# Pooling stage: order of low parts, evictions and value tiles; end of the delta rule: places of the inverses, token halves of the first output tiles

## What is computed

```python
def rms_norm(x, g):
    xf = x.astype(jnp.float32)
    return xf * lax.rsqrt(jnp.mean(xf * xf, axis=-1, keepdims=True) + EPS) * g

def multiscale_pool(h, w_groups, scale):            # windows 2, 4, 8, 16, one for each 256 channels
    hf = h.reshape(B, L, POOL_GROUPS, POOL_G)
    ...                                             # d = mean over the last w tokens, less the token
    return jnp.einsum("blgc,gce->blge", d, w_groups).reshape(B, L, D) * scale

def gated_delta_rule(q, k, v, a, b, a_log, dt_bias):
    """S_t = a_t S_{t-1} (I - beta_t k_t k_t^T) + beta_t v_t k_t^T, o_t = S_t q_t (chunkwise form)."""
    ...
    sol = triangular_solve(lower + eye, rhs)        # rhs = [v * beta, k * beta * exp(G)], u, w = sol
    def step(state, xs):
        v_new = u_n - einsum("bhcd,bhde->bhce", w_n, state)
        o_n = einsum("bhcd,bhde->bhce", qg_n, state) + einsum("bhij,bhje->bhie", p_n, v_new)
        state = state * gl_n + einsum("bhcd,bhce->bhde", kg_n, v_new)
        return state, o_n

def second_block(x, mem, ...):
    mem_n = rms_norm(mem, mem_norm)
    u = rms_norm(h, norm_pre_mix)
    y_mix, q_mem = gdn_branch(u @ gdn_w_in, ...)    # delta rule, rms_norm of each head, times silu(z)
    mem_k, mem_v = jnp.split(mem_n @ w_mem_kv, 2, axis=-1)
    y_mem = memory_attention(q_mem, mem_k, mem_v)
    y = jnp.concatenate([y_mix, y_mem], axis=-1) @ w_out
    h = h + rms_norm(y, norm_post_mix)
    return h + rms_norm(swiglu(rms_norm(h, norm_pre_ffn), w_ffn_in, w_ffn_out), norm_post_ffn)
```

## Time and profile before

| | |
|---|---|
| median of three runs | 1973.01 us (1971.21 to 1976.17) |
| the profiled execution, device time | 1976.93 us |
| its span, first to last instruction | 1975.1 us |
| PE, DVE, ACT busy | 1918.6, 1021.8, 771.5 us |
| mean granted clock of PE | 0.989 of full speed |
| DMA, mean | 82 GB/s |

### The profile page before, as it was taken

How to read it: one execution, slowest core, us unless ns; L and a number is a source line. 1 busy time by engine, 2 the same in 40 slices (tenths; PEclk the granted TensorE clock), 3 DMA queues, 4 the chain that set the end, 5 groups by cost and what they waited for, 6 DMA issues and landing times.

```text
span 1975.1 us, 28804 instructions
## 1 busy us (share of the span) xinstructions
PE 1918.6 (97%) x11532; PEld 1679.3 (85%) x11532; DVE 1021.8 (52%) x1459; ACT 771.5 (39%) x1255; POOL 32.7 (2%) x31
## 2 busy tenths in 40 slices
PE   7999998999999998999999999999999999999997
PEld 7888788999999998888888877787898888888886
DVE  5654475564444454454444468678546354333335
ACT  5345443342222344433232333635675452222332
POOL 0100000100000000000000000000000000000000
PEclk9999999999999999999999999999999999999998
DMA  5221101232322232222222322222102222223321
GB/s 186 66 65 43 57 1 44 86 101 87 96 86 94 89 94 87 95 91 91 96 96 96 96 92 90 75 65 79 60 1 96 86 84 89 95 86 107 96 85 54
DMA packets 47177, 162.20 MB, mean 82 GB/s; under 512 B 5368, under 2 KB 7672, under 8 KB 46936
## 3 DMA queue, kind: packets, MB, share of 16 engines
q1 hardware_dynamic: 46208, 158.60, 24.9%
q10 hardware_dynamic: 856, 2.00, 0.3%
HBM read 156.38 MB, written 4.19 MB: 81 GB/s over the span
## 4 chain that ended last, share of the span: by engine, by line
PE 91%; DVE 4%; ACT 3%; DVEq 1%; issue 1%; DMA 0%; SPq 0%; ACTq 0%
PE ps L456 78%; PE ps L998 2%; PE ps L867 1%; PE ps L1018 1%; PE ps L585 1%; PE ps L843 1%; DVE wlo L2290 1%; DVE AM L2469 1%; PE ps L845 1%; PE ps L564 0%; PE ps L565 0%; ACT WU L1989 0%; PE ps L1003 0%; PE ps L858 0%; PE ps L1129 0%
## 5 line engine op out<-in xcount | busy, mean ns | idle before, releaser
L456 PE MATMUL ps<-UH,whi 128*128 128x264 f32 (+2 forms) x1904 | 645.7, 339 | 10.5 <-DVE wlo L2290 9.4
L456 PE MATMUL ps<-UL,whi 128*128 128x264 f32 (+2 forms) x1904 | 637.1, 335 | 0.0
L456 PE MATMUL ps<-UH,wlo 128*128 128x264 f32 (+3 forms) x1616 | 521.7, 323 | 0.0
L1468 ACT ACTIVATE whi<-raw 128x1024 fp32r<-128x1024 f32 x284 | 297.9, 1053 | 438.7 <-PE ps L456 418.7
L456 PEld LDWEIGHTS ps<-UH,whi 128*128 128x128 f32 x1904 | 358.5, 188 | 52.0 <-issue 12.8
L456 PEld LDWEIGHTS ps<-UL,whi 128*128 128x128 f32 x1904 | 358.4, 188 | 39.4 <-issue 2.4
L2290 DVE TENSOR_TENSOR wlo<-raw,whi 128x1024 fp32r<-128x1024 f32 x248 | 308.1, 1246 | 53.0 <-ACT whi L1468 52.7
L456 PEld LDWEIGHTS ps<-UH,wlo 128*128 128x128 f32 (+1 forms) x1616 | 303.5, 188 | 24.5
L456 PE MATMUL ps<-HH,whi 128*128 128x264 f32 (+1 forms) x768 | 246.4, 321 | 0.0
L456 PE MATMUL ps<-HL,whi 128*128 128x264 f32 (+1 forms) x768 | 246.3, 321 | 0.0
L456 PE MATMUL ps<-HH,wlo 128*128 128x264 f32 (+1 forms) x768 | 245.7, 320 | 0.0
(11 more groups left out here) (450 smaller groups left out, 2378.7 us busy)
## 6 DMA issues: line engine op xcount, KB each, us to landing
raw<-W SPq DMA_DIRECT2D x284, 512.0 KB, 3.5
H<-xT SPq DMA_DIRECT2D x4, 528.0 KB, 6.8
spill<-H SPq DMA_DIRECT2D x1, 2048.0 KB, 9.1
H<-spill SPq DMA_DIRECT2D x1, 2048.0 KB, 9.7
MEM<-memT ACTq DMA_DIRECT2D x1, 1024.0 KB, 4.9
out<-H SPq DMA_DIRECT2D x2, 512.0 KB, 2.9
out<-H SPq DMA_DIRECT2D x4, 256.0 KB, 3.2
masks<-masks SPq DMA_DIRECT2D x1, 768.0 KB, 10.2
```

The costliest lines, as they stand in the source:

```text
L456: mm = pe.matmul(dst, a, b, start=start and n == 0, stop=stop_ and n == 2)
L1468: act.activation(whi[s % NB][:, :, :], raw[s % NB][:, :, :], ACT.Copy).then_inc(w_hi, 1)
```

## The change

Pooling: `MEM_ORDER` has the value tiles `m4` to `m7` first and the key tiles last; the packed weights follow (`MEM_HEADS`). PE transposes the values ahead of the third-last memory tile (`m2`), no longer behind the last. ACT converts the two slots that take the buffers of the pool's weights in the middle of the evictions of `UV` (`pool_weights_read`), and does each `input_hi` ahead of the next `memory_out`. DVE makes those two low parts ahead of the first `pool_out`, and one instead of three further ones stands in its way.

End of the delta rule: chunk c's inverse lies in buffer (c + 2) mod 4 (`blocks_at`), so chunks 0 and 1 are in the buffers of the first two output slots; `squares` moves out of `whi`'s first buffer. ACT converts slot `wout2 + 2` early, DVE makes the low parts of `wout2` and `wout2 + 1` together. `heads_part` takes a half of the tokens and a set of heads; PE's order at the end is new, the two groups of transposes of a chunk 2 or 3 use different banks, and ACT's last steps are reordered. The core of the diff:

```diff
-MEM_ORDER = ["m0", "m1", "p0", "p1", "m2", "p2", "p3", "m3", "p4", "p5", "m4", "p6", "p7", "m5", "m6", "m7"]
+MEM_ORDER = ["m4", "m5", "p0", "p1", "m6", "p2", "p3", "m7", "p4", "p5", "m0", "p6", "p7", "m1", "m2", "m3"]
...
+def blocks_at(c):
+    return GH * ((c + 2) % 4)
...
-        squares, = region(scratch, ("squares", [P, GH, P], F32))
+        squares, = region(r_at + L * 4, ("squares", [P, GH, P], F32))
...
+                if name == "m2":
+                    memory_values_turned()
...
-                turned(2 if c < 2 else 3, lambda x: YG[g][:, x, :]).then_inc(G["ot"], 1)
+                turned(2 if c < 2 else 3 - 2 * g, lambda x: YG[g][:, x, :]).then_inc(G["ot"], 1)
...
+            def heads_part(e, half, heads):
+                t = TILE0["wout2"] + e
+                pe.wait_ge(w_lo, head_blocks // SLOT + e + 1)
+                pe.wait_ge(G["lo"], 8 if half and 4 in heads else 7 if half else 4)
+                c = slice(half * NMEM, (half + 1) * NMEM)
+                for k in heads:
+                    wh, wl = block_at(head_blocks + GH * e + k)
+                    mm = passes(psum(t, SEQ)[:, c], wh, wl, YH[:, k, c], YL[:, k, c], False, half == 1 and k == GH - 1)
...
             solved(3, 1)
-            memory_part(0)
             within(3, 0)
-            within(3, 1)
             pe.wait_ge(G["pt"], 8)
             outputs_turned(2, 0)
+            memory_part(0, (0,))
+            within(3, 1)
+            outputs_turned(2, 1)
+            memory_part(0, (1, 2, 3))
+            heads_part(0, 0, (0, 1, 2, 3))
             pe.wait_ge(G["gt"], 5)
-            outputs_turned(2, 1)
-            memory_part(1)
+            outputs_turned(3, 0)
+            heads_part(0, 0, (4, 5, 6, 7))
             pe.wait_ge(G["gt"], 6)
-            outputs_turned(3, 0)
-            pe.wait_ge(G["gt"], 7)
             outputs_turned(3, 1)
-            heads_part(0)
-            heads_part(1)
+            memory_part(1, (0, 1, 2, 3))
+            heads_part(1, 0, range(GH))
+            for e in range(2):
+                heads_part(e, 1, (0, 1, 2, 3))
+                heads_part(e, 1, (4, 5, 6, 7))
...
+            def pool_weights_read(n):
+                s = Head.slot
+                act.wait_ge(raw_in[s % NB], 16 * (s // NB + 1))
+                act.wait_ge(part_done, KT + n)
+                act.activation(whi[s % NB][:, :, :], raw[s % NB][:, :, :], ACT.Copy).then_inc(w_hi, 1)
+                Head.slot += 1
...
             pool_windows()
+            pool_weights_read(5)
             for n in range(6, 12):
                 pool_values(n)
+            pool_weights_read(11)
+            memory_out(4)
+            memory_out(5)
+            input_hi(0)
+            memory_out(6)
+            input_hi(1)
+            memory_out(7)
+            input_hi(2)
             memory_out(0)
+            input_hi(3)
             memory_out(1)
-            memory_out(2)
-            input_hi(0)
...
-            weights_hi(0, to=wout2 + 2)
+            weights_hi(0, to=wout2 + 3)
...
             solved(3, 0)
+            solved(3, 1)
             queries_out(3, 1)
-            solved(3, 1)
+            gated_hi(2, 0)
             rstd_heads(3, 0)
-            gated_hi(2, 0)
+            gated_hi(2, 1)
             rstd_heads(3, 1)
-            gated_hi(2, 1)
+            gated_hi(3, 0)
+            gated_hi(3, 1)
             act.wait_ge(G["kv"], 6)
             weights_hi(0, to=wout2 + 4)
-            gated_hi(3, 0)
-            gated_hi(3, 1)
...
             weights_lo(0, to=BLOCK0["mem"] // SLOT + NB)
-            weights_lo(MEM_TILE["m0"])
-            weights_lo(MEM_TILE["m1"])
+            weights_lo(0, to=BLOCK0["mem"] // SLOT + NB + 2)
             pool_out(0)
             pool_out(1)
-            weights_lo(MEM_TILE["m2"])
+            weights_lo(MEM_TILE["m5"])
             input_lo(0)
...
-            dve.wait_ge(G["y"], 6)
-            weights_lo(0, to=wout2 + 1)
+            dve.wait_ge(G["y"], 4)
+            weights_lo(0, to=wout2 + 2)
...
-            dve.wait_ge(G["y"], 8)
-            weights_lo(0, to=wout2 + 2)
+            dve.wait_ge(G["y"], 6)
+            weights_lo(0, to=wout2 + 3)
```

92 lines of the change are left out of this document (44 added, 48 removed).

## The result

The changed kernel takes 1956.09 us (median of four runs, 1954.81 to 1959.46), the kernel before beside it 1973.58 us: ratio 0.9908, 95% interval 0.9892 to 0.9923, so 15.2 to 21.3 us less. The forecast was 1955.6 us, 17.4 us less; 17.5 us less was measured. The profiled execution took 1957.04 us, its span is 1955.2 us, 19.9 less than the span of before.

The account below looks back on a forecast made before the run. PE, busy 97% of the span, was taken as the bound, with waits and low clock in two places. Pooling 10.7 plus delta rule's end 6.7 made 17.4 us; 1973.0 - 17.4 = 1955.6 us, range 1951 to 1962.

Parts of the forecast that it names:

- (a): Pooling: evictions still stand behind the input's low parts, waits and clock stay, only the end gains; 1965.3 us, chance 0.07.
- (b): Delta rule's end: longer chain, PE waits twice 1.5 us, 3 to 4.5 us come back; 1959 to 1960, chance 0.10.
- (c): Pooling and delta rule's end: the clock falls without the waits, three falls stay; 1961.5 us, chance 0.06.
- (d): Delta rule's end: the token halves' weight loads are not hidden, costing 9.0 us; 1964.6 us, chance 0.02.
- (e): Pooling: clock goes low early and stays low up to the second MLP, slower than before; 1984.5 us, chance 0.02.
- The walk of the order: Pooling: new order followed with old durations; low parts done before evictions, no PE wait, 32.82 us in place of 43.48.
- The margin of DVE: Pooling's steady state: DVE's low parts are done by 773.7, the next pooled tile ends at 774.3; 0.6 us.
- switches: Delta rule's end: the first matmul behind each of six switches is slower, 0.5 us added in all.
- The wait of 0.25 before `within(3,1)`: Delta rule's end: `within(3,1)` starts near 1504.9 with 0.25 us of wait, raising the stretch from 21.8 to 22.0.
- The norms: Delta rule's end: chunk 3's two norms ready at 1509.1 and 1511.6, PE asks at 1509.9 and 1511.9.
- The second token half: Delta rule's end: PE has work to 1518.0, chunk 3's low parts end at 1514.8; 3.2 us of slack.
- the last `residual`: Before the last solve: DVE's extra low part delays it by about 0.2 us against some 0.5 of slack.

Follow-up runs that it names:

- high_parts_late: The changed kernel with ACT making each input block's high parts behind the next memory tile's eviction and weight conversion again; 1968.38 us, ratio 0.9966.
- before_pooling_filled: The kernel before with sixteen unused 256-column matmuls on PE ahead of each of the three waiting memory tiles; 1972.72 us, ratio 1.0001.

## Why the prediction was right

**The sum.** Forecast 17.4 us and 1955.6, measured 17.5 and 1956.09. The halves of the sum held apart as well: 10.7 against 10.3 for pooling (6.9 to 13.4), 6.7 against 6.7 (3.8 to 9.5). None of the rivals happened: no eviction behind low parts (a), no long chain (b), no fall inside the two places (c), in this trace or in any other that has the new order there, no cost of the halves (d), no low clock through pooling (e).

**Pooling.** The walk of the order held: low parts done before the eviction, no wait, the values' transposes free, weight slots in time. ACT's order was named as what decides, and high_parts_late shows that the waits come back without it. Sizes: the stage was forecast at 32.82 us and took 32.33. A pair of pooled tiles costs PE 2.15 (765.15 to 767.30), not 2.34: that was the shown duration up to the modelled end of the last matmul, not the spacing to the next. Four pairs make 0.76 too much; the memory tiles behind short work cost up to 2.9 rather than 2.83, 0.3 in all the other way. The margin of DVE was given as 0.6 us and was 0.85 to 0.9. The weak step is the clock: the 10.7 took the falls of one execution (1.5 us twice) as if each run had them. Without any fall the waits and the slow first matmuls behind them cost 8.0 us (40.33 - 32.33, from before_pooling_filled), and 4 falls in 10 waits add 1.2 x 1.6 = 1.9, so about 9.9 was the value to expect of a mean run; the measurement, 6.9 to 13.4, does not tell it from 10.7.

**The end of the delta rule.** Forecast 22.0 us, taken 21.07. By terms: solve 0.90 (0.8), `within` 1.81 (1.78), four turns 0.36 each and 1.45 in all (1.76), memory heads 5.82 (5.6), halves 11.09 (11.3 and 0.5 for switches). The halves are 0.1135 apart, not 0.118. The 0.118 was read rightly from the two memory tiles, which have no switch in them and take 5.66 us after the change too; matmuls of this width come at either spacing, and which one was not foreseen. The wait of 0.25 before `within(3,1)` did not come: ACT's last step for it ended at 1492.15, and PE asked at 1492.35. The norms were ready at 1496.58 and 1498.91 and asked for at 1497.17 and 1499.06: 0.59 and 0.15 us of slack, where I gave 0.8 and 0.3. The second token half was asked for at 1505.04, its low parts ended at 1501.87: 3.2 us, as forecast. Nothing showed at the last `residual`: the last two solves are 2.68 us apart before and after. That the 6.7 us agree exactly is luck: the new stretch came out 0.9 us shorter than forecast, and the old one, counted as 28.71, took 28.71, 28.70 and 27.47 in the three traces that have it, again by the clock. That the placement costs nothing was right; that it also brings nothing (0.16 us) I had not said.

**The rivals' prices.** (c) and (e) were weighed by waits and by the mix of short groups alone. The runs show two roads to a fall: falls behind waits, and a fall in a stream with no wait. (d) was rejected for the right reason, but the reason was thinner than it read: at 256 columns the matmul is longer than the floor of its load by 2 ns.

## What to carry to other kernels

When an engine off the critical path serves two chains in turn, ask first which of its instructions stands in front of the one that a third engine waits for: here the place of four short ACT steps decided over all three repeated waits. The halves of a product split along its free dimension are a good filler for a tail of dependent steps, as long as each piece takes longer than its weight load. Price a wait by its length, and its fall of the clock by how often it occurs over several traces, not by the one trace at hand.
